# Gate and up products moved directly behind the preceding down product, in all experts but the first and last

## What is computed

```python
g_idx = jnp.argmax(g_logits, axis=-1)            # one of 4 groups of experts
top_val, top_idx = lax.top_k(e_logits, EXPERT_TOPK)   # 2 of its 8 experts
gate = jax.nn.softmax(top_val, axis=-1) * g_w[:, None]
...
hid = jax.nn.silu(xblk @ w_gate[e]) * (xblk @ w_up[e])
return hid @ w_down[e]
...
y = jnp.zeros((n_tok + 1, d), ht.dtype).at[tok_buf].add(out * w_buf[:, None])
```

## Time and profile before

| | us |
|---|---|
| median of 3 runs | 1425.46 (1425.19 to 1426.78) |
| the profiled execution, its own time | 1428.13 |
| its span (first to last instruction) | 1426.3 |
| PE busy in the span | 1211.8 (85%) |
| DVE busy | 593.4 (42%) |
| ACT busy | 210.2 (15%) |
| mean granted clock of TensorE | 0.916 |
| read from HBM | 474.63 MB |

### The profile page before, as it was taken

How to read it: one execution, slowest core, us unless ns; L and a number is a source line. 1 busy time by engine, 2 the same in 40 slices (tenths; PEclk the granted TensorE clock), 3 DMA queues, 4 the chain that set the end, 5 groups by cost and what they waited for, 6 DMA issues and landing times.

```text
span 1426.3 us, 16078 instructions
## 1 busy us (share of the span) xinstructions
PE 1211.8 (85%) x6731; PEld 565.9 (40%) x6731; DVE 593.4 (42%) x1221; ACT 210.2 (15%) x461; POOL 14.0 (1%) x31
## 2 busy tenths in 40 slices
PE   8999999999999999887767877877777688777877
PEld 4884566556884543322222222222222223222223
DVE  5999985757843443332122322222122212123122
ACT  3311023342022320110000100000000000000001
POOL 3000000000000000000000000000000000000000
PEclk9999999999999998998777998898898978889789
DMA  9344445233566779999999999999999999999998
GB/s 290 134 148 150 156 166 199 96 118 114 183 240 197 304 296 427 396 429 432 431 429 432 431 428 431 429 433 431 429 434 426 432 433 428 434 428 428 436 424 314
DMA packets 62728, 477.79 MB, mean 335 GB/s; under 512 B 13701, under 2 KB 21253, under 8 KB 45504
## 3 DMA queue, kind: packets, MB, share of 16 engines
q1 hardware_dynamic: 61392, 476.40, 81.0%
q0 software_dynamic: 864, 0.25, 0.3%
q10 hardware_dynamic: 400, 0.10, 0.0%
HBM read 474.63 MB, written 2.11 MB: 334 GB/s over the span
## 4 chain that ended last, share of the span: by engine, by line
PE 52%; DMA 33%; DVE 8%; ACT 3%; SPq 2%; issue 1%; DVEq 0%; ACTq 0%
DMA ring<-in_moe_w_up_dram 20%; PE bank L1293 12%; PE bank L734 11%; DMA late_ring<-in_moe_w_up_dram 9%; PE bank L1328 7%; PE bank L1050 5%; PE bank L1252 3%; PE bank L1314 2%; DMA late_ring<-in_moe_w_down_dram 2%; PE bank L1019 2%; PE bank L1178 2%; PE bank L1365 2%; DMA ring<-in_moe_w_down_dram 2%; PE bank L718 1%; PE bank L1134 1%
## 5 line engine op out<-in xcount | busy, mean ns | idle before, releaser
L1293 PE MATMUL bank<-ring,x_gathered 128*32 128x512 f32 x1184 | 256.8, 693 | 58.2 <-DMA late_ring<-in_moe_w_up_dram 35.2
L1293 PE MATMUL bank<-late_ring,x_gathered 128*32 128x512 f32 x800 | 204.8, 689 | 35.0 <-DMA ring<-in_moe_w_up_dram 33.6
L2732 DVE TENSOR_TENSOR tokens_out<-tokens_out,bank 128x512 f32<-128x512 f32 x240 | 148.6, 681 | 191.5 <-PE bank L1365 191.5
L734 PE MATMUL bank<-ring,hT 128*128 128x512 f32 (+2 forms) x416 | 156.1, 536 | 2.2 <-ACT hT L1565 2.0
L2715 DVE SCALAR_TENSOR_TENSOR hidden<-hidden,bank 128x128 f32<-128x128 f32 x31 | 8.9, 288 | 352.5 <-ACT hidden L1881 352.5
L1293 PEld LDWEIGHTS bank<-ring,x_gathered 128*32 128x32 f32 x1184 | 67.4, 125 | 148.8 <-issue 145.9
L1252 PE MATMUL bank<-x_tok,select 128*32 128x512 f32 x512 | 115.9, 1033 | 7.3 <-DVE select L2624 4.2
L734 PEld LDWEIGHTS bank<-ring,hT 128*128 128x128 f32 x416 | 78.7, 190 | 76.3 <-issue 66.8
L1328 PE MATMUL bank<-ring,hidden 128*32 128x512 f32 x560 | 92.2, 818 | 18.2 <-DVE hidden L2717 18.2
L1293 PEld LDWEIGHTS bank<-late_ring,x_gathered 128*32 128x32 f32 x800 | 53.5, 124 | 111.0 <-issue 108.5
L1365 PE MATMUL bank<-y_slots,weight_slots 32*128 32x512 f32 x496 | 72.5, 654 | 29.5 <-ACT y_slots L1896 21.7
(11 more groups left out here) (464 smaller groups left out, 1213.5 us busy)
## 6 DMA issues: line engine op xcount, KB each, us to landing
ring<-in_moe_w_up_dram SPq DMA_DIRECT2D x19, 4096.0 KB, 39.1
ring<-in_moe_w_down_dram SPq DMA_DIRECT2D x16, 4096.0 KB, 29.7
ring<-in_moe_w_gate_dram SPq DMA_DIRECT2D x16, 4096.0 KB, 38.5
late_ring<-in_moe_w_down_dram SPq DMA_DIRECT2D x13, 4096.0 KB, 29.2
late_ring<-in_moe_w_gate_dram SPq DMA_DIRECT2D x12, 4096.0 KB, 39.4
late_ring<-in_moe_w_up_dram SPq DMA_DIRECT2D x10, 4096.0 KB, 40.7
ring<-in_w_in_dram SPq DMA_DIRECT2D x20, 1024.0 KB, 8.1
ring<-in_w_out_dram SPq DMA_DIRECT2D x16, 1024.0 KB, 6.5
```

Source lines behind the costliest of these rows:

```text
L734: mm = pe.matmul(b, lhs(i)[:, P * tt:P * tt + P], piece_view(key)[:, c, at:at + cols], start=i == 0, stop=i == n - 1)
L1293: mm = pe.matmul(gu_bank[SLOTS * c:SLOTS * c + SLOTS, :], XGT[:, at, n % 4, n // 4, :], pieces[c % 2][:, FF * (n % 8):FF * (n % 8) + FF], ...
L2732: ins = v.tensor_tensor(y, x, mix[c][:, :], ALU.add)
```

## The change

In `straight`, the four parts of `gate_up` of expert j move from behind the combination of j - 1, the gather and turning of the rows of j + 1 and the turning of the weights of j, to ahead of them, directly behind the down product of j - 1. That holds for experts 2 to 7 of the head (1 had that order already) and for main's j = 1 to 21, experts 10 to 30. Experts 0, 9 (main's j = 0), the loop's 8 and the last, 31, keep their order. No instruction is added or dropped, and the other engines' programs keep their order, SP's too.

```diff
-                if f is head and j == 1:
+                if j and not (f is main and j == last):
                     for i in range(4):
                         gate_up(f, j, i, j % 2, arrived_at, place[2 * (i // 2):2 * (i // 2) + 2])
-                    wait_task(pe, "tab")
+                    if f is head and j == 1:
+                        wait_task(pe, "tab")
                 if j:
                     combine(f, j - 1, 0)
...
-                if f is not head or j > 1:
+                if j == 0:
                     for i in range(4):
                         gate_up(f, j, i, j % 2, arrived_at, place[2 * (i // 2):2 * (i // 2) + 2])
                 turn_hidden(f, j)
```

## The result

The changed kernel takes 1430.47 us (median of 12 runs, 1428.57 to 1437.64), against 1425.97 us for the kernel before (12 runs, 1424.14 to 1428.71). The ratio is 1.0033, with a 95% interval of 1.0021 to 1.0045: slower by 4.7 us, between 3.0 and 6.4. The profiled execution took 1431.08 us, with a span of 1429.2, which is only 2.95 us more than that of before (1428.13).

A forecast was written before the change was run, and what follows sets the result against it. The prediction took the stream of weight loads, plus TensorE's work after the last weights land, to bound the kernel. Its terms, -3.1 + 5.1 + 2.5 = +4.5 us, gave a median of 1430.0 us, range 1424 to 1434.

The forecast's parts named there:

- part D: At the end, expert 30's down product starts later and expert 31's DMA waits absorb only some: +2.5 us.
- the stretch near 580: Dry load queue from 579.4 to 582.5 us, as SP issues only after expert 2's gate and up: 3.1 us lost.
- part C: Experts 10 to 30: down starts 6.5 us later, but up loads keep 25.6 us of margin, so no cost.
- Part A: Expert 2's gate and up run earlier, SP issues at 573.9 and the dry queue near 580 goes: -3.1 us.
- Part B: Expert 7's down product starts later, so the loop's gate load is issued late and the queue runs dry: +5.1 us.
- The forecast's high end: At the loop, expert 7's down product at 6.26 us adds 2.6, for a dry stretch of 6.8 us.
- Rival 1: Expert 7's path grows by 1.4 us or less, no dry queue at the loop: -0.6 us, 1424.9; chance 0.14.
- rival 4: Something else holds expert 2's gate and up, so the dry queue near 580 stays: +7.6 us, 1433.1; chance 0.05.
- Rival 2: TensorE stays at full clock through back-to-back products, at expert 7, loop and expert 30: -3.1 us, 1422.4; chance 0.10.
- Rival 3: TensorE still later, a second dry stretch at main's first expert: up to +9.1 us, 1434.6; chance 0.09.
- The fixed cost of some 2.0 us: The skill's fixed cost per DMA transfer; if it held, the loop's dry stretch and the sum would be 1.8 us smaller.

The follow-up runs named there:

- Experts 2 to 6 alone: Only experts 2 to 6 take the new order, 7 and main as in the kernel before: ratio 0.9991 to the kernel before.
- with the loop's load cut: Experts 2 to 6 in the new order, the loop's gate load split into two 2 MB loads: 0.9985 to the kernel before, 1424.50 us.
- Head alone: Only experts 2 to 7 take the new order, main as in the kernel before: ratio 1.0006 to the kernel before.
- before (second): The unchanged kernel before, profiled once more: 1425.64 us for that execution.
- products added: The kernel before with three useless products around the turning of expert 1's hidden rows, to hold TensorE's clock up: ratio 0.9998.
- main alone: Only experts 10 to 30 take the new order, the head as in the kernel before: ratio 1.0023 to the kernel before.
- 10 to 29: Only experts 10 to 29 take the new order, head, expert 30 and end as in the kernel before: ratio 0.9997.
- before (first): The unchanged kernel before, in the first trace, from which the forecast was made: 1428.13 us for that execution.
- expert 30 alone: Of experts 2 to 30 only expert 30 takes the new order, the rest as in the kernel before: ratio 1.0014.
- expert 7 alone: Of experts 2 to 30 only expert 7 takes the new order, the rest as in the kernel before: ratio 1.0026.
- the control: The kernel before with only the loop's gate load cut in two, no gate and up moved: ratio 0.9997.

## Why the prediction was right, point by point

**The forecast.** +4.5 us was forecast and 4.7 (3.0 to 6.4) measured; the forecast and not a rival came in. The mechanisms of parts A to D are all seen. That the sum met the figure so closely is partly luck, since its first term was sized on an execution that is not the usual one, and the clock ran otherwise than was taken.

**The two traces.** The forecast for the profiled execution was 1432.6, and it took 1431.08. Of the 2.95 us between the two, 1.6 come from the front, which leaves 1.4 for the change. The forecast's own terms with what the trace after shows give -3.1 + 4.9 + 0.7 = 2.5, where 0.7 is part D with a down product at full clock; the other 1.1 is what expert 30's gate and up took less, 8.54 instead of 9.65 us, which no term foresaw. The medians differ by 4.5 all the same: the trace of before is one with the stretch near 580, and by the table above it stands in three of seven such traces.

**What bounds the kernel.** Right: the stream of loads from 620 on, and the end. Twenty experts moved inside the stream cost nothing (0.9997), which confirms that part C costs nothing.

**Part A, -3.1 us.** The mechanism was right: the issue at 573.6 with the offset taken off, against a forecast of 573.9, and the stretch gone. The step that failed is the one that took the stretch as a fixed property of the kernel before. It stands in 3 of the 7 traces with the old order and no added product. Where it stands it cost some 2.5 us: the two traces of before start expert 1's down product within 0.1 us of each other and took 1428.13 and 1425.64 us. Part of the 2.5 can be the clock at the end. By 3/7 of 2.5 to 3.1 the mean gain would be about 1.1 to 1.3 us, a rough estimate from seven traces. Experts 2 to 6 alone gave 1.3 (-0.3 to 2.9), with 1.4 us lost at the loop in its trace, and with the loop's load cut 2.1 (0.4 to 3.7), which takes in the 3.1. So the mean gain is not settled between these.

**Part B, +5.1 us.** The loop's issue was forecast at 748.5 and came at 748.6 with the offset taken off, the dry stretch at 5.1 and measured 4.9. Two small errors met in it. The path of expert 7 was forecast at 9.5 us and measured 9.3, and its down product started at 716.9 with the offset taken off, 0.4 earlier than the 717.3 forecast. And of the down product's lower clock half was counted, 0.9 us, where all of it came through: it took 1.4 us more than at full clock, and from its start to the loop's gate load are 31.7 us against 30.3 before, with the slow loop unchanged (8.04 and 8.02 us for its 48 products).

That rule, that a slower down product makes the loop's load later by as much, is wrong at its other end. Head alone has the same order up to the loop:

```profile
717.56 6.50 PE bank L1329 x32
...
738.96 5.36 PE bank L1294 x48
```

Expert 7's down product was still slower there, and the loop behind it ran at full clock: 29.2 us from one to the other, 2.5 less than after, and 2.8 us dry instead of 4.9. The forecast's high end had this case at +2.6. All traces in which the loop's gate load is one load fall into three groups, whatever the order of expert 7 (durations by the timeline, which gives some 0.05 us less than the chain):

| down of expert 7, us | traces | from its start to the loop's gate load, us |
|---|---|---|
| 6.34 to 6.46 | before (second), products added, main alone, 10 to 29, head alone | 29.1 to 29.2 |
| 3.64 | before (first), expert 30 alone | 30.3 |
| 4.97 to 5.22 | after, expert 7 alone, experts 2 to 6 | 31.7 to 31.9 |

So the cost of part B depends on where in this stretch the clock changes, and one trace does not give its mean. Expert 7 alone costs 3.7 us (2.1 to 5.3), which takes in the 5.1; the cut of one load gives the changed kernel 4.7 back. That it is this load's lateness, and not the later down products elsewhere, is shown by that pair and the control, as far as their intervals of some 2 us go.

**Part D, +2.5 us.** Alone it gave +2.0 (0.1 to 3.8). The waits that take up the delay went, as forecast. In the changed kernel's trace the down product ran at full clock, 3.64 and not the 5.4 taken. The size for each clock was not tested.

**Sum of the parts.** -1.3 + 3.7 + 2.0 = +4.4 by the runs of the parts, against -3.1 + 5.1 + 2.5 = +4.5: by the middle values part A was 1.8 us too large as a gain and parts B and D together 1.9 too large as a loss, which took each other away. Each of the three has an interval of some 1.6 to 1.9 us to either side, so only the miss of part A is borne out, and that by the traces. The head and main alone add to 0.9 + 3.3 = 4.2, near the 4.7 of both.

**Rivals.** Rival 1 (the loop's margin holds) and rival 4 (the stretch near 580 stays) are ruled out for the changed kernel by its windows. Rival 2, the full clock throughout, did not come: expert 7's gate and up took 9.15 us and its down product 5.06, with the wait for the weights where it was. The advice of the Trainium skill (Perfetto Trace Analysis, "Matmul Optimizations") to run products back to back in batches is not met by an order alone where the engine waits for DMA, here 7.00 us ahead of expert 7's gate and up. Rival 3 did not come either: the window from 790 to 795 moved 426 GB/s. Some share of the executions may have it; one took 1437.64 us and has no trace, so that stays open. The fixed cost of some 2.0 us (the Trainium skill, DMA: Bandwidth & Descriptors, "Anatomy of one DMA") is stated there for transfers that GpSimd issues, while SyncE issues the loads here. The trace of after speaks for the 1.4 and 2.4 us from rows 3 and 5: the dry stretch measured 4.9, not 3.3.

## What to carry to other kernels

Where the loads bound a kernel, an order of products is worth only what it does to the moments at which buffers come free, so look for the few places where the queue is nearly empty: here one expert of 27 made the loss at the loop, one the loss at the end, and 20 did nothing. Cutting the load that is late there gave back 4.7 us. And before a gain is counted from one trace, take a second one of the same kernel and ask whether what it removes is there again. The time of the profiled execution against the median is no guide to that. Expert 30 alone has the stretch near 580 in its trace, at 1428.64 us with a median of 1428.68. The changed kernel with the cut load has no dry stretch in its trace and took 1431.09 with a median of 1427.16; there the front was late, since expert 1's down product starts at 563.32 instead of 560.20. So count from a point behind the part that the change leaves alone.

## What the runs showed of the hardware that was not expected

The granted clock of one down product differs between executions of the same kernel: that of expert 1, starting at 560.20 and at 560.26 us, took 6.51 us at half clock in one and 3.64 in the other, with the same work ahead of it. These 2.9 us go with a queue of loads that runs dry or does not, and the two executions ended 2.5 us apart. A slower product does not always mean a later end: where expert 7's down product took 6.4 us at half clock, the 48 products of the loop behind it took 5.36 us, and where it took 3.64 or some 5 us they took 8.0 to 8.3. The front varies too: the trace of after lies 1.6 us behind that of before, and between 263 and 268 us it has windows at a clock of 0.73 and 0.67 where before has 1.00. That this is what made the 1.6 us was not tested.
